# Branch A's column sums placed earlier, its plain tiles gated in place, token splits placed later, in a hybrid linear-attention and window-attention block

## What is computed

```python
(q_a, k_a, v_a, lr_a, z_a, q_b, k_b, v_b, z_b, m_a, m_b) = split_cols(einsum(h, w_in))
# branch A: gated linear attention, chunks of 64 tokens
S = S * exp(b_last) + k_dec.T @ v          # per chunk and head
o = q @ S
ga = rmsnorm(o) * silu(z_a);   y_a = ga @ w_branch_gla
# branch B: window attention with rotary positions and a sink per head
gb = softmax_window(q_b, k_b, v_b) * silu(z_b);   y_b = gb @ w_branch_swa
y = sigmoid(m_a + ba) * y_a + sigmoid(m_b + bb) * y_b
out = x + rmsnorm(y @ w_out)
```

## Time and profile before

| | |
|---|---|
| median of 3 runs | 2000.07 us (1998.47 to 2007.79) |
| the profiled execution's own time | 1996.81 us |
| its span, first to last instruction | 1994.9 us |
| PE busy | 1909.8 us (96%) |
| DVE, POOL, ACT busy | 1439.0, 1056.2, 880.1 us |
| granted TensorE clock, mean | 0.986 |
| DMA | 416.06 MB, 209 GB/s over the span |

### The profile page before, as it was taken

One profiled execution on the slowest core, in us unless ns is written; L12 is line 12 of the kernel. 1 busy time (PEld: TensorE's weight loads), 2 busy tenths in 40 slices (PEclk: granted clock), 3 DMA queues, 4 the chain that ended last, 5 costly groups with the idle time before them and its releaser, 6 DMA issues. The chain is left out here.

```text
span 1994.9 us, 29306 instructions
## 1 busy us (share of the span) xinstructions
PE 1909.8 (96%) x9876; PEld 1524.8 (76%) x9876; DVE 1439.0 (72%) x2219; ACT 880.1 (44%) x1929; POOL 1056.2 (53%) x671
## 2 busy tenths in 40 slices
PE   8999999999999998899999999999999988999896
PEld 7778877777777776777878777777777767777785
DVE  6768876976767667788488887856676676886363
ACT  5457465443444442334267345443444442335421
POOL 5634464644433356668444455553433475768744
PEclk9999999999999998999999999999999999999998
DMA  7524375666776688976433557644767598885862
GB/s 270 167 68 141 116 236 168 217 214 209 227 240 215 198 290 271 349 252 219 146 101 102 166 168 236 216 148 152 224 201 253 182 327 275 311 283 164 309 228 85
DMA packets 280246, 416.06 MB, mean 209 GB/s; under 512 B 33507, under 2 KB 159011, under 8 KB 265635
## 3 DMA queue, kind: packets, MB, share of 16 engines
q1 hardware_dynamic: 280099, 414.20, 63.2%
HBM read 272.10 MB, written 142.02 MB: 208 GB/s over the span
## 5 line engine op out<-in xcount | busy, mean ns | idle before, releaser
L938 PE MATMUL pu<-a_hi,w_hi 128*128 128x512 f32 x1964 | 779.9, 399 | 39.0 <-DVE ct L1839 16.4
L938 PE MATMUL pu<-a_hi,w_lo 128*128 128x512 f32 x1964 | 764.6, 391 | 0.4 <-POOL w_lo L1954 0.4
L938 PE MATMUL pu<-a_lo,w_hi 128*128 128x512 f32 x1964 | 764.0, 391 | 0.0
L1954 POOL TENSOR_TENSOR w_lo<-t,w_hi 128x512 fp32r<-128x512 f32 x276 | 396.5, 1445 | 439.7 <-ACT w_hi L1278 439.4
L1954 POOL TENSOR_TENSOR w_lo<-w_raw,w_hi 128x512 fp32r<-128x512 f32 x259 | 385.1, 1497 | 292.6 <-ACT w_hi L1278 292.5
L938 PEld LDWEIGHTS pu<-a_hi,w_hi 128*128 128x128 f32 x1964 | 370.3, 189 | 137.1 <-issue 57.1
L938 PEld LDWEIGHTS pu<-a_hi,w_lo 128*128 128x128 f32 x1964 | 370.4, 189 | 80.4 <-POOL w_lo L1954 0.8
L938 PEld LDWEIGHTS pu<-a_lo,w_hi 128*128 128x128 f32 x1964 | 370.9, 189 | 72.7
L1278 ACT ACTIVATE w_hi<-t 128x512 fp32r<-128x512 f32 x276 | 170.5, 630 | 208.9 <-DVE t L497 147.5
L1963 POOL TENSOR_TENSOR a_lo<-fill_in,a_hi 128x1024 fp32r<-128x1024 f32 x52 | 141.3, 2718 | 107.3 <-ACT a_hi L1297 107.3
L1278 ACT ACTIVATE w_hi<-w_raw 128x512 fp32r<-128x512 f32 x259 | 158.1, 630 | 21.8 <-PE pu L938 16.7
(11 more groups left out here) (186 smaller groups left out, 2465.9 us busy)
## 6 DMA issues: line engine op xcount, KB each, us to landing
w_raw<-in_w SPq DMA_DIRECT2D x81, 1024.0 KB, 7.0
va_d<-ct SPq DMA_DIRECT2D x32, 256.0 KB
qb_d<-ct SPq DMA_DIRECT2D x32, 256.0 KB
zb_d<-ct SPq DMA_DIRECT2D x32, 256.0 KB
q_s<-qb_d SPq DMA_DIRECT2D x32, 256.0 KB, 3.8
z_s<-zb_d SPq DMA_DIRECT2D x32, 256.0 KB, 3.1
gb_d<-gb SPq DMA_DIRECT2D x32, 256.0 KB, 3.6
za_d<-ct SPq DMA_DIRECT2D x32, 256.0 KB
```

What stands on the lines that cost most here:

```text
L938: return nc.tensor.matmul(dst, weights, moving, start=start, stop=stop, skip_group_check=True)
L1954: TT(flat(w_lo[o.n % NWB][:, :, :]), src, as_f32(flat(w_hi[o.n % NWB][:, :, :])), ALU.subtract) \
```

## The change

1. Fills: all eight are split later against the stage's start, by one slot (A11, A12, S3) or two (the others), and six of them (all but A11 and A12) are loaded one or two slots later.
2. Sum jobs of kind gb stand 8 slots apart instead of 10. Two of the four ga jobs move forward into the mA groups, with place-0 buffers, at slots 184 and 191 of the pass (22 and 15 ahead of the yB stage); the other two stand at slots 12 and 20 of the yB stage. The fill of A11 for yB waits for the stores of all place-0 jobs, since their buffers lie in the same memory.
3. The plain yA tiles: the product of bank and gate is written over the gate tile, with no wait for `ct`; the addition of `yb` into `ct` comes one slot later and has that wait. Store and the next gate load come one slot later.
4. The norm of pass 0's output: partition sums at slot 6 and 7 of the last stage instead of 3 and 4, spreading at 11 instead of 6, first tile at 13 instead of 9.

No instruction is added or removed.

```diff
-    for _name, _load, _split, _free in (("A11", -10, -6, -7), ("A12", -9, -5, -6), ("A21", -5, -2, -5),
-                                        ("A22", -4, -1, -4), ("S2", -1, 2, -3), ("S1", 0, 3, -2), ("S3", 3, 7, 6),
-                                        ("S4", 4, 9, -1)):
+    for _name, _load, _split, _free in (("A11", -10, -5, -7), ("A12", -9, -4, -6), ("A21", -4, 0, -5),
+                                        ("A22", -3, 1, -4), ("S2", 0, 4, -3), ("S1", 1, 5, -2), ("S3", 5, 8, 6),
+                                        ("S4", 6, 11, -1)):
...
-SUMS = 3
-RB_END = 6
-NORM = {9 + x: x for x in range(16)}
+SUMS = 6
+RB_END = 11
+NORM = {13 + x: x for x in range(16)}
...
-    _jobs = [("gb", BASE[0] + 152 + 10 * j, 0) for j in range(KH)]
-    if _sb:
-        _jobs = [("y", BASE[1] + 82 + 10 * j, 0) for j in range(KH)] + [("gb", BASE[1] + 150 + 10 * j, 0)
-                                                                        for j in range(KH)]
-    _jobs += [("ga", YBASE[_sb] + 4 + 6 * j, 1) for j in range(KH)]
+    _jobs = [("y", BASE[1] + 82 + 10 * j, 0) for j in range(KH)] if _sb else []
+    _jobs += [("gb", BASE[_sb] - 2 * _sb + 152 + 8 * j, 0) for j in range(KH)]
+    _jobs += [("ga", BASE[_sb] - 2 * _sb + 184 + 7 * j, 0) for j in range(2)]
+    _jobs += [("ga", YBASE[_sb] + 12 + 8 * j, 1) for j in range(2)]
...
+def stage_jobs(sb):
+    return max(j.n for j in SUM_JOBS if j.place == 0 and j.first < YBASE[sb]) + 1
...
-                        sp.wait_ge(gs_out, 16 * 4 * jobs_done(f.sb, "gb"))
+                        sp.wait_ge(gs_out, 16 * 4 * stage_jobs(f.sb))
...
+                if job.what == "ga":
+                    sp.wait_ge(ga_out, 16 * (16 * job.sb + 8 * (job.j // 2 + 1)))
...
-                    if g and g.n and not g.fast and g.n in STORED:
+                    if g and g.n and not g.fast and g.n in STORED and g.kind != "yA":
+                        store_tile(g, n)
+                for g, n in ((step(s, lag), n) for n, lag in ((0, 3), (1, 5), (2, 7), (3, 9))):
+                    if g and g.kind == "yA" and not g.fast:
                         store_tile(g, n)
...
-                    if e == YA_AT + 2 * n + 2:
+                    if e == YA_AT + 2 * n + 3:
                         load_gate_a(sb, 1, n)
...
-                        ct_free(dve, g, c)
-                        STT(ct[c][:, :], gate_a[c][:, :], 1.0, bank[:, :], ALU.add, ALU.mult).then_inc(ya_ok, 1)
-                        dve.wait_ge(ya_ok, 4 * g.sb + c + 1)
-                        TT(ct[c][:, :], ct[c][:, :], yb[c][:, :], ALU.add).then_inc(y_ok, 1)
+                        STT(gate_a[c][:, :], gate_a[c][:, :], 1.0, bank[:, :], ALU.add, ALU.mult).then_inc(ya_ok, 1)
+                for c in range(4):
+                    g = step(s, 2 * c + 2)
+                    if g and g.kind == "yA" and not g.fast:
+                        dve.wait_ge(ya_ok, 4 * g.sb + c + 1)
+                        ct_free(dve, g, c)
+                        TT(ct[c][:, :], gate_a[c][:, :], yb[c][:, :], ALU.add).then_inc(y_ok, 1)
```

More of the change, by code:

```diff
@@ L712, in load_sums @@
                             sp.wait_ge(h_out, 16 * 7 * KH)
-                    elif job.what == "ga":
-                        sp.wait_ge(ga_out, 16 * 16 * (job.sb + 1))
-                    else:
+                    elif job.what == "y":
                         stored(group_no(0, "yA", 3))
```

## The result

| | before | after |
|---|---|---|
| median of 7 runs each | 2000.07 us | 1987.47 us (1980.46 to 1992.75) |
| profiled execution, its own time | 1996.81 us | 1985.35 us |
| its span | 1994.9 us | 1983.2 us |
| ratio of the medians | | 0.9933, interval 0.9908 to 0.9957 |

The change wins 12.6 us by the medians and 11.5 by the two profiled executions. The forecast was 39.4 less; 1987.47 lies above the upper end of 1980. The sign was right, the size three times too large.

What follows compares the result with a forecast made beforehand. PE was taken to bound the kernel, with 67.6 us of idle time and low clock in five windows; 28.2 us would stay or come, so 39.4 less: 1957.4 profiled, 1960 for the median. The range was 1940 to 1980.

Steps and rivals of the forecast that it cites:

- m groups: In the m groups, each of four moved sum jobs costs 0.6 us of PE waiting, 2.4 us in both passes.
- Sum jobs, slots 12 and 20: In yB, two remaining jobs take 5 to 7 us of DVE each, covered by the rest of a group's 19 us.
- Splits later: Late fill chain leaves S3 waits with clock loss: 8.4 us in yB, 11.4 in yA, 3.5 in v and out.
- DMA decides: Fill transfer times set the result: below the forecast if no fill is late, above if each is as slow as the slowest.
- S3's times in yB and yA of pass 0: S3 ready at 757.3 in yB, about 850.9 in yA: waits 2.5 and 3.0 us, plus 1.7 clock loss each.
- yA in place: In yA, the second gate no longer waits for a store, so 9.5 us of PE waiting in two go.
- Norm: In the last stage, the sums move three slots, 8.2 us, so the 5.79 us wait on `acc` goes; 0.5 us stays.
- A: Rival: no fill is late, so the six waits on S3 go; median about 1940; chance 0.18.
- B: Rival: the store wait moves to yA's addition, delaying S2 and S3 by 3 us; median 1974; chance 0.22.
- C: Rival: slower, as A21, S2 and S3 transfers all take 11.5 us in six stages; 2034; chance 0.04.
- D: Rival: waits only move, with S3, A22 and DVE's backlog taking as much; 1990 to 2005; chance 0.06.

Runs made afterwards that it cites:

- No_additions: Changed kernel with fills at their old places and the yB sum jobs' additions one column wide, so its output differs: 1972.56 us, one run.
- S3_at_8: early_fills with the split of S3 alone one slot later, at slot 8: 1983.75 us, ratio 0.9907 to the kernel before.
- ya_only: Kernel before with only the plain yA tiles multiplied in place: 2001.4 us against 2002.0, ratio 0.9999.
- sums_only: Kernel before with only the sum jobs placed as in the change: 1991.7 us against 2002.0, ratio 0.9944.
- norm_and_sums: Kernel before with only the later norm and the moved sum jobs, yA and fills as before: 1979.5 us against 2000.5, ratio 0.9890.
- loads_after: Changed kernel with old fills, yB additions one per slot, and jobs ahead of yB 6 slots earlier, 8 apart: 1982.3 us, ratio 0.9903 to the kernel before.
- fills_only: Kernel before with only the fills loaded and split as in the change: 2018.9 us against 2002.0, ratio 1.0085.
- mixed_fills: Changed kernel with late fills in yB and yA alone, old places elsewhere: 1981.9 us, ratio 0.9893 to the kernel before.
- early_fills: Changed kernel with all fills loaded and split at their old places: 1981.2 us against 2003.3 for the kernel before, ratio 0.9889.
- s3_at_7: Changed kernel with the split of S3 alone one slot earlier, at slot 7: 1995.5 us, ratio 0.9968 to the kernel before.

## Why the prediction was wrong, point by point

The sum holds stage by stage, so each of its terms can be set beside the lengths of the table (us, length less the length without waits):

| stages | before | forecast to stay | after |
|---|---|---|---|
| yB 0, yB 1 | 14.1, 14.7 | 5.2, 5.2 | 11.3, 14.5 |
| yA 0, yA 1 | 10.9, 8.7 | 5.7, 5.7 | 6.6, 6.9 |
| v and out 0 | 4.4, 6.3 | 3.5 together | 7.0, 7.5 |
| out 1 | 9.7 | 0.5 | 0 |
| m groups, change | | +2.4 | +2.6 |

- **Sum jobs, slots 12 and 20: the step that failed.** I wrote "cover being the rest of a group's 19 us" and costed the two jobs at nothing. What counts isn't a group's length but the next deadline on DVE's list, and L1909 stands right behind the job's second slot. It cost 5.10 and 6.5 us, with the clock two slots of 9.53 and 11.96 us where 2.72 were due: 6.8 + 9.2 = 16.0 us, as much as the 15.4 us by which yB fell short. No_additions, where DVE's work for these jobs is nearly gone, has no wait on L1909. The row that would have told it was there: a job's four additions take 6.60 us, 1.65 each, where the gate of the same shape in the next row takes 0.68, and I didn't ask why, nor add up what stands between the job and L1909. The Trainium skill (SBUF — State Buffer, SBUF: two separate sides) says that a DVE instruction with two SBUF inputs and a GpSimd instruction that reads SBUF contend, and that the one that came second is fully blocked meanwhile. The rows agree: 1.74 to 1.77 us against 0.68, and operations that read a bank stay at 0.68. So a DVE operation of this form is to be priced at some 1.7 us where POOL works through its `w_lo`, and it can be more: L499 took 2.88 at 911.72, beside POOL's split of a fill.
- **Splits later: reason and size failed.** For v and out I gave S3's place behind the bank copy as the reason and 3.5 us as what stays; 10.7 stood before and 14.5 are there now. So 7.2 us that I had booked as won by the change didn't come, and 3.8 were added. S3_at_8 shows that place to be worth 0.1 and 1.2 us of wait. The chain A21, S2, S3 is what went late: by 4 us at A21's half on DVE, behind yA's last tiles, and in v again at S2's copy on ACT, behind a bank copy that waits for a store. I had "S2 and then S3 are issued later" for yB, and walked neither DVE's nor ACT's list at the start of v and out. In yB of pass 1 a late split also kept the wait on L1857 that I had said would go (2.3 us).
- **"DMA decides": wrong.** S3's transfers in yB and yA of pass 0 took 7.8 and 8.4 us, close to the 8 and 9.5 taken, so the loads were no slower than I thought; the time was lost in the order of work on DVE and ACT.
- **S3's times in yB and yA of pass 0: right.** Issued at 745.66 (I took 744.8), split from 753.50 (752.8), done on POOL at 758.3 (757.3); its transfer took 7.8 us, 8 taken. In yA of pass 0 the issue is at 835.6, the landing at 844.0, 8.4 us where I took 9.5. The waits are 2.43 and 0.82 us in the two yB (2.5 taken), 1.73 and 1.92 in the two yA (3.0), and the clock fell only behind the first of the four, where I had charged 1.7 us for each. The rows, from the changed kernel:

```profile
753.50 2.01 ACT L1304 ACTIVATE a_hi<-fill_in 128x1024 fp32r<-128x1024 f32 x2 [1.28 <-DMA fill_in<-s_gb_S]
...
755.65 2.67 POOL L1973 TENSOR_TENSOR a_lo<-fill_in,a_hi 128x1024 fp32r<-128x1024 f32 x1 [1.25 <-ACT a_hi L1304]
```

- **yA in place: right in its sign, wrong in its worth.** The 9.5 us of the second gate were booked as won by this edit. Alone it wins nothing (ya_only), and without it the wait shrinks to 1.4 to 2.6 once the jobs leave yB (sums_only, norm_and_sums). The wait on the store was real, but DVE was late at that gate anyway. That the stage came out near the forecast (6.6 and 6.9 against 5.7) is luck: the clock's loss that I had charged didn't come, and waits that I had not came instead (1.4 us on L1868, 1.5 on L1921 in pass 0).
- **Norm: right.** 9.9 us were forecast for that stage, 9.7 came.
- **m groups: right in size by luck, not in place.** The jobs cost no wait on L1839, as I took from the earlier trace rows, but waits on `d_g`, loads of the attention behind `gx` on SP (loads_after): 4.8 us in five.
- **Rivals.** A is out, since PE still waits 0.8 to 2.4 us on S3 in yB and yA. B is out: the addition in yA doesn't hold S2, S3's issue comes 18.3 us after the stage's start, where I took 18.6. C is out, with no wait on S3 over 5.2 us; yet fills_only shows that the later fills alone do land on the slow side, with PE waiting on the gates and sums of DVE, not on slow transfers. D (1990 to 2005) comes nearest, 2.5 us below its range, and its list (S3, A22, DVE's backlog) names the right places. It deserved more than 0.06: I had walked the lists only as far as the old waits, and had no row for what stood behind them.

What stays open: the medians of mixed_fills and early_fills agree within 0.7 us while their profiled executions differ by 9, so the cost of late fills in yB and yA alone lies somewhere between. And v and out 0 still hold 11 us with early fills (in v 1.5 us of waiting on L1480 and 2.0 on `u`, with the clock at 1.00 from 935 to 945 us, behind the latter); what would take those away wasn't tried.

## What to carry to other kernels

When a job leaves a stage or moves in it, write down the list of its engine up to the next operation that another engine waits for, with the duration that each operation has beside what runs then, and compare with that deadline; a group's spare time is no cover. When splits or copies move later, walk the list of every engine that holds them, stage by stage, for the first instruction there that waits on something else: that one sets the new time. And measure the parts of a bundle alone: here two of four carried the gain (1979.5 us), one did nothing, and one cost some 9 us beside the others.

## What was unexpected of the hardware

- A DVE operation of 128x512 with both inputs in SBUF took 0.68 us with POOL idle and mostly 1.74 to 1.77 beside its `w_lo`, up to 2.9 beside its splits; POOL's own `w_lo` of that size took 1.25 and 1.7 to 1.9. Even additions of 128x1 took 1.1 to 1.2, and 0.16 with POOL idle. It isn't so every time: in no_additions L1908 took 0.68 at 768.95 with POOL at work.
- The length of a wait didn't tell what it cost in clock. Four windows of the changed kernel, around waits of PE of 1.73, 2.43, 5.10 and 6.50 us:

```profile
849.00:856.00 7.00, 5.41 (x24) 4.52 (x25) 6.06 (x7) 3.20 (x5) 5.45 (x5) 1.00 0.66 223
760.00:767.00 7.00, 7.00 (x26) 5.57 (x25) 5.13 (x4) 3.57 (x5) 5.44 (x4) 0.76 0.54 196
773.00:784.00 11.00, 6.53 (x22) 5.30 (x23) 7.22 (x11) 2.27 (x4) 3.82 (x3) 0.84 0.65 221
1654.00:1665.00 11.00, 9.14 (x29) 7.37 (x30) 5.60 (x10) 1.64 (x3) 2.45 (x2) 0.69 0.73 244
```

and one each of s3_at_7, around a wait of 3.69 us, and of early_fills, around one of 2.23:

```profile
938.00:947.00 9.00, 6.42 (x28) 5.37 (x29) 6.70 (x7) 3.75 (x6) 7.45 (x5) 1.00 0.41 145
851.00:860.00 9.00, 6.85 (x23) 5.52 (x24) 8.79 (x7) 1.68 (x3) 9.00 (x6) 0.81 0.57 152
```

After 1.73 us the clock stayed at 2.4 GHz, and the product took 4.71 = 2.72 + 1.73 + 0.26. After 2.43 it was partly at 1.2 GHz, 7 x 0.24 = 1.7 us lost; after 5.10, 11 x 0.16 = 1.8; after 6.50, 11 x 0.31 = 3.4. But after 3.69 nothing was lost, and after 2.23 there were 9 x 0.19 = 1.7. So a short wait can cost as much clock as one of twice its length, or none, and whether it does was not the same from one kernel to the next at waits of some 2 to 4 us. For a wait of that size a forecast can say 0 or some 1.7 us, and not more finely from the length alone.
